# A two-layer hybrid diffusion step on one core: the second half of the first shift ahead of the first half products, and four weight casts behind the last feature tile

## What is computed

```python
mod_p = ada_params(c_ctx[None, :], w_mod[layer], b_mod[layer])   # silu(c) @ w_mod + b_mod, six parts
hs = modulate(rmsnorm(xs, norm_mix_pre[layer]), mod_s[0], mod_s[1])   # x * (1 + scale) + shift
# even layer
u, v, gate, xr = jnp.split(h @ w_in, [D_A, 2 * D_A, 2 * D_A + D_RG], axis=-1)
ya = chunk_gmlp(u, v, gm_g, gm_ws, gm_bs)
yb, fin = rglru_mixer(xr, gate, h0, conv_w, conv_b, wa, ba, wi, bi, lam)
return jnp.concatenate([ya, yb], axis=-1) @ w_out, fin
```

## Time and profile before

| what | value |
|---|---|
| median of three runs | 1608.98 us (1607.75 to 1613.0) |
| the profiled execution | 1612.72 us, its span from the first to the last instruction 1610.4 us |
| TensorE busy | 1496.5 us, 93% of the span |
| VectorE, ScalarE, GpSimd busy | 657.9, 550.0 and 512.2 us |
| mean granted clock of TensorE | 0.969 |
| moved by DMA | 153.87 MB, mean 96 GB/s |

### The profile page before, as it was taken

How to read it: one execution, slowest core, us unless ns; L and a number is a source line. 1 busy time by engine, 2 the same in 40 slices (tenths; PEclk the granted TensorE clock), 3 DMA queues, 4 the chain that set the end, 5 groups by cost and what they waited for, 6 DMA issues and landing times.

```text
span 1610.4 us, 20091 instructions
## 1 busy us (share of the span) xinstructions
PE 1496.5 (93%) x8338; PEld 1241.8 (77%) x8338; DVE 657.9 (41%) x1128; ACT 550.0 (34%) x910; POOL 512.2 (32%) x219
## 2 busy tenths in 40 slices
PE   4899979899999999999789789989899999999998
PEld 3786646787898899897667656657699889989985
DVE  4475663632323222232834466624532222223225
ACT  4347723631131232222531265524532223222311
POOL 1322133243143243232324134413343324323330
PEclk8999979999999999999899899999899999999999
DMA  9313434234343222134142000034232122213221
GB/s 340 125 53 107 155 101 161 66 118 156 109 154 106 79 80 77 55 103 157 51 164 79 27 1 1 1 105 131 81 116 79 54 77 80 78 55 103 79 81 76
DMA packets 90546, 153.87 MB, mean 96 GB/s; under 512 B 6404, under 2 KB 44752, under 8 KB 90456
## 3 DMA queue, kind: packets, MB, share of 16 engines
q1 hardware_dynamic: 82432, 145.76, 27.4%
q10 hardware_dynamic: 8024, 6.83, 1.5%
HBM read 149.69 MB, written 2.89 MB: 95 GB/s over the span
## 4 chain that ended last, share of the span: by engine, by line
PE 41%; DVE 4%; ACT 3%; DMA 1%; issue 1%; POOL 1%; DVEq 0%; ACTq 0%; SPq 0%
PE PS L1223 11%; PE PS L1224 11%; PE PS L1225 11%; PE PS L1497 2%; PE PS L1489 1%; PE PS L1467 1%; PE PS L1450 1%; PE PS L1275 1%; POOL WL L893 1%; PE PS L1468 1%; DVE RAW L537 1%; DVE GG L1188 1%; ACT WH L663 1%; ACT GG L850 1%; DMA RAW<-in_w_mod 1%
## 5 line engine op out<-in xcount | busy, mean ns | idle before, releaser
L893 POOL TENSOR_TENSOR WL<-RAW,WH 128x1024 fp32r<-128x1024 f32 x170 | 418.0, 2491 | 754.5 <-ACT WH L663 754.5
L1223 PE MATMUL PS<-HH,WH 128*128 128x384 f32 (+1 forms) x1152 | 360.2, 313 | 12.5 <-DVE HL L1046 7.9
L1224 PE MATMUL PS<-HL,WH 128*128 128x384 f32 (+1 forms) x1152 | 358.4, 311 | 0.0
L1225 PE MATMUL PS<-HH,WL 128*128 128x384 f32 (+1 forms) x1152 | 357.9, 311 | 0.0
L663 ACT CAST WH<-RAW 128x1024 fp32r<-128x1024 f32 x170 | 168.3, 1046 | 484.9 <-PE PS L1225 338.5
L1223 PE MATMUL PS<-WH,AH 128*128 128x512 f32 x640 | 251.8, 393 | 7.8 <-DVE ACC L1144 7.8
L1225 PE MATMUL PS<-WH,AL 128*128 128x512 f32 x640 | 250.4, 391 | 0.0
L1224 PE MATMUL PS<-WL,AH 128*128 128x512 f32 x640 | 250.3, 391 | 0.0
L1223 PEld LDWEIGHTS PS<-HH,WH 128*128 128x128 f32 x1152 | 221.1, 192 | 17.9 <-issue 10.7
L1224 PEld LDWEIGHTS PS<-HL,WH 128*128 128x128 f32 x1152 | 221.1, 192 | 0.8 <-issue 0.3
L1225 PEld LDWEIGHTS PS<-HH,WL 128*128 128x128 f32 x1152 | 220.9, 192 | 0.0
(11 more groups left out here) (173 smaller groups left out, 1549.2 us busy)
## 6 DMA issues: line engine op xcount, KB each, us to landing
RAW<-in_w_mod SPq DMA_DIRECT2D x43, 1024.0 KB, 5.2
RAW<-in_w_ffn_in SPq DMA_DIRECT2D x32, 1024.0 KB, 5.6
RAW<-in_w_ffn_out SPq DMA_DIRECT2D x32, 1024.0 KB, 4.8
RAW<-in_w_in_even SPq DMA_DIRECT2D x7, 1024.0 KB, 5.4
RAW<-in_w_qkv SPq DMA_DIRECT2D x6, 1024.0 KB, 5.3
RAW<-in_w_out_even SPq DMA_DIRECT2D x4, 1024.0 KB, 5.4
RAW<-in_w_out_odd SPq DMA_DIRECT2D x4, 1024.0 KB, 5.1
X<-in_x_sample SPq DMA_DIRECT2D x4, 512.0 KB, 6.2
```

The source lines that it names most:

```text
L893: nc.gpsimd.tensor_tensor(ring_view(WL, ld, j), w_view(ld, b), ring_view(WH, ld, j).bitcast(f32), ALU.subtract).then_inc(w_lo, 1)
L1223: MM(out, wh, xh, start=first, stop=False)
L1224: MM(out, wh, xl, start=False, stop=False)
L1225: return MM(out, wl, xh, start=False, stop=last)
```

## The change

The whole difference lies in `schedule()`:

```diff
     flush()
     for f in range(4):
         step("h0", f=f)
+    mod(0, 0, 1)
     step("A0", i=0, j=0)
-    mod(0, 0, 1)
     mod(0, 1, 1)
     flush()
     step("A0", i=1, j=0)
     for f in range(4, KD):
         step("h0", f=f)
-        steps[-1]["split"] = {5: [2], 6: [3], 7: [4, 5]}.get(f, [])
+    steps[-1]["split"] = [2, 3, 4, 5]
     apair("xr", 0, ("w_in",), 1536, None, ld, kh=1)
```

## The result

The changed kernel took 1600.53 us (median of seven runs, 1597.19 to 1604.77) against 1610.62 us for seven runs of the kernel before (1607.75 to 1615.65). The ratio is 0.9931, with a 95% interval of 0.9914 to 0.9948: 11.1 us less, between 8.4 and 13.8. A second set of runs of both kernels gave 0.9953 (0.9937 to 0.9968), 7.6 us less, between 5.1 and 10.1. (In that set eight executions of the changed kernel took 1599.4 to 1601.7 us and four took 1606.8 to 1607.1, so the two medians lie 9.2 us apart; no trace shows one of the slower four.) The direction and the time (1600.8) were right, but that the time fits to 0.3 us is in part luck: the traces show 10.1 us gained in the stretch that the change touches, where the sum said 8.2, and the kernel before now has a median 1.6 us above the one that the forecast started from. The two errors cancel.

The account below looks back on a forecast made before the run. The prediction took TensorE's stream, its idle times and lower clock, to bound the kernel. Gains of 2.4 + 5.8 = 8.2 us off the 1608.98 us median gave 1600.8 us, range 1596.5 to 1606.

Parts of the forecast that it names:

- What bounds it: Whole kernel: TensorE's stream, busy 93% of 1610.4 us; its gains reach the end unless a later wait takes them.
- Part one: Half products mod(0, 0, 1) moved ahead of A0 (i=0), into TensorE's 3.30 us idle time: gain 2.4 us.
- The 0.3 us by which A0 was to start later: A0's start behind the moved half products: 34.6 to 34.9 instead of 34.41, cost 0.2 to 0.5, taken as 0.3 us.
- rival B: A0's products: TensorE's clock rises earlier, near 37, 2.0 us more, total gain 10.2, time 1598.8 us; chance 0.16.
- the sign that the prediction had set for B: At A0 (i=0): A0 ended near 39.
- Part two: Casts 2 to 5 behind h0 7: 5.8 us, 4.1 from VectorE held by GpSimd, 1.7 from the half-clock stretch.
- The thin lead of HL 7 over the first remainder: At h0 7: VectorE's HL 7 ahead of GpSimd's first remainder by about 1 us, one cast.
- The covers: Moved steps finish before TensorE wants them: first bank by 0.7 us, bank behind the nine transfers by 1.1 us.
- rival D: Behind the second features: a thin cover is missing, overrun 1 to 3 us, time 1601.8 to 1603.8; chance 0.06.
- Rival C: At HL 7: GpSimd's remainder begins first and holds it; part two worth 0.8 to 2.5 us, total 3.2 to 4.9; chance 0.12.
- Rival E: A0 behind the wait for load 6: past 33 us each microsecond late costs one; slower, chance 0.04 with all else.
- The chances: Whole kernel's time: faster 0.80, same 0.16, slower 0.04; the forecast itself 0.62.

Follow-up runs that it names:

- gated kernel: Kernel before, casts unmoved; only GpSimd waits, ahead of its remainder for block 2, until all eight HL are made; ratio 0.9965, 5.6 us less.
- kernel with three gates: Changed kernel plus three GpSimd waits, at blocks 18, 88 and 109; ratio to the kernel before 0.9929, then 0.9931 (1600.05 us).
- kernel with one cast early: Changed kernel with block 2 alone cast behind h0 6, blocks 3 to 5 behind h0 7; ratio to the kernel before 0.9962, 6.1 us less.

## Why the prediction was right, and where it was not

**What bounds it.** Right. What TensorE's stream had gained at the fourth xr tile in the first pair of traces (10.1 us, counted from the first cast of h0) was still there at 160 us (10.2) and at the last tile's norm (10.0). Between executions of one kernel, though, that last anchor differs by 3.0 and 5.5 us (1571.6 and 1568.6 before; 1561.7, 1559.1 and 1556.1 changed), so that one pair can't show the end to a microsecond. One reason seen is that the clock falls in a later idle stretch or doesn't: 0.78 and 0.88 of full in 84 to 89 and 89 to 94 us in the first trace of the changed kernel and 1.00 in the second, worth 1.6 us. The two timings, 11.1 and 7.6 us, lie on either side of 10.1 within that scatter.

**Part one, the sum 3.32 - 0.58 - 0.3 = 2.4.** The order did what was said: half products in the gap, only the transposes behind A0 (38.30 to 38.83, 0.53 us). Two terms were off. The 0.3 us by which A0 was to start later did not come in the first trace: load 6 let the second group start at 31.8, the clock rose at 32.2, and A0 began at 33.62, which is 34.41 less the 0.79 us by which this trace is earlier. In the second trace, where the clock rose later, the half products took 3.64 us and A0 began at 34.61, 0.2 us late, as the term has it. The term that mattered is A0's own length, carried over from before as 6.5 us, as if its products kept the half clock. It was 4.7 us here, since the HL of its feature tiles and not a slow clock now hold it. This is rival B, given 0.16 and priced at 2.0 us more (its own figures, 41.2 less 39.0, give 2.2); in the first pair of traces it was 1.8 + 0.3, and A0 ended at 38.30 + 0.79 = 39.1 in the time of the kernel before, the sign that the prediction had set for B. The clock rose at 33.0 in that time, sooner than the 37 of rival B. The argument against B, that half products are thin work for bringing the clock back, is the step that failed. How much it costs the sum varies: 6.5 us was the longest of four, and in the other three traces with that order there was less to gain.

**Part two, 5.8.** Right in cause and size: 5.5 us against the first trace of the kernel before, 6.3 against the second, where the stretch at half clock was longer (its products ran at half clock from 55.9 to 61.0, 5.1 us, where it was 3.15). That the cause is GpSimd's exclusion of VectorE and not ScalarE's order is shown by the gated kernel. The thin lead of HL 7 over the first remainder (about 1 us was said) held: HL 7 began by 48.4 and ended at 49.22, the remainder began at 49.39.

**The covers.** The copy of the first xr tile, said to be covered by 0.7 us, stood at 52.06 and was done 1.2 us before TensorE wanted its bank at 54.0. The copy behind the nine transfers, covered by 1.1 us, was done at 66.8 for a bank wanted at 68.1. These rows of the changed kernel's ScalarE and its queue answer to the earlier trace rows:

```profile
59.60 1.05 ACT L663 CAST WH<-RAW 128x1024 fp32r<-128x1024 f32 x1 [4.91 <-DMA RAW<-in_w_in_even]
...
65.47 0.62 ACTq L745 DMA_DIRECT2D HF<-in_gmlp_ws  x1
66.13 0.69 ACT L750 COPY MX<-PS 128x640 f32<-128x640 f32 x1 [3.01 <-issue]
68.10 0.69 ACT L750 COPY MX<-PS 128x640 f32<-128x640 f32 x1 [1.28 <-PE PS L1225]
```

ScalarE now waits 4.91 us for load 11, and its copy at 66.13 waits for its own queue instead of for TensorE, as worked out; rival D did not occur by 1.3 us. Rival C did not occur; brought about by one early cast, it cost 3.6 us in the trace, inside its price of 3.3 to 5.0 (the part of 5.8 that it was to take). Rival E did not occur: the wait for load 6 ended before 32. In the first trace of the kernel with three gates the second group waited for that load until 33.72, and A was still 9.11.

**The chances.** Added up as the prediction says, its cases give 0.85 for faster and 0.11 for the same, not 0.80 and 0.16; nothing else rests on it.

## What to carry to other kernels

Where VectorE and GpSimd both work in SBUF, look for a VectorE instruction that suddenly takes twice its usual length or more (here 2 to 14 times) and ends with one of GpSimd's. It may be held, and letting GpSimd wait a little tests that: here one wait was worth 5.6 us. Put work that must be done anyway, and doesn't depend on what TensorE is waiting for, into the wait. Its worth can be more than its own length, through the clock of the products behind it: here 3.4 to 4.6 us in the traces, where the order by itself was put at 2.4. Before a duration at half clock is carried into a sum, look at a second execution: the same 24 products took 5.2 to 6.5 us.

## What the runs showed of the hardware

With thin products (32 weight columns) ahead of A0, TensorE's clock came back from 1.2 to 2.4 GHz sooner. Read off from stretches of one microsecond, the clock was at full 3.0 to 6.0 us after the start of the transposes ahead in eight traces that have them, and 7.8 to 10.6 us after it in the four that don't. In the first trace of the changed kernel it rose at 32.2, before A0's first product (33.62), when nothing but half products and transposes had run. (In the first trace of the kernel with three gates it had fallen only at 30.0, just ahead of the transposes; in the other eleven it was already at half at 28.) The stretch in which it rose in the kernel before, and the one in the changed kernel's third trace:

```profile
40.00:41.00 1.00, 1.00 (x8) 0.76 (x11) 0.00 (x0) 0.00 (x0) 0.00 (x0) 0.71 0.04 12
```

```profile
35.00:36.00 1.00, 1.00 (x6) 0.92 (x7) 1.00 (x3) 0.73 (x1) 0.00 (x0) 0.82 1.05 379
```

A small instruction is held as long as a large one. Two of 128x8 elements that take 0.17 us alone took 2.34 and 2.29 us in the kernel with one cast early, which is the length of one remainder (2.35 us) each time. Together with HL 7 just ahead of them (2.73) they read as the two engines taking turns, one instruction each.

```profile
52.88 2.34 DVE L961 TENSOR_SCALAR LG<-PC 128x8 f32<-128x8 f32 x1
55.25 2.29 DVE L962 TENSOR_TENSOR LG<-PC,LG 128x8 f32<-128x8 f32 x1
```

In that kernel an idle time of 1.77 us was followed by 3.4 us at half clock; the changed kernel's idle times of 0.24 and 0.30 us in the same place were not. The idle time alone doesn't settle it: ahead of its first products of line 1363 (at 97.89 us in the kernel before, 87.00 in the changed kernel) TensorE stands idle for 2.7 us, and there the clock fell in the first trace of either kernel (at 98.4 and 86.8 us) and stayed at full in the second trace of either.
